# A second buffer for the transposed rope pages, and the next entry's page transposes ahead of the score mask

## The reference, cut to what matters

```python
c_past = cache_kv_latent[i][page_table].reshape(db, past, KV_LORA)
kr_past = cache_k_rope[i][page_table].reshape(db, past, ROPE_DIM)
s_past = einsum('bthc,bsc->bhts', q_abs, c_past) + einsum('bthr,bsr->bhts', q_rope, kr_past)
s = concatenate([s_past, s_new], -1) * scale          # s_new: the new token itself
p = softmax(s)
o_lat = einsum('bhts,bsc->bthc', p[..., :past], c_past) + einsum('bhtu,buc->bthc', p[..., past:], c_new)
```

## Time and profile before

| | |
|---|---|
| median of 3 runs | 1068.41 us (1066.91 to 1068.78) |
| span of the profiled execution | 1064.8 us; the profile gives no other time for that execution |
| PE busy | 990.8 us, 93% of the span |
| VectorE busy | 668.9 us, 63% |
| ScalarE busy | 387.6 us, 36% |
| GpSimd busy | 69.0 us, 6%, nearly all of it the gathers |
| chain that ended last | PE 78%, VectorE 12%, ScalarE 2% |

### The profile page before, as it was taken

How to read it: one execution, slowest core, us unless ns; L and a number is a source line. 1 busy time by engine, 2 the same in 40 slices (tenths; PEclk the granted TensorE clock), 3 DMA queues, 4 the chain that set the end, 5 groups by cost and what they waited for, 6 DMA issues and landing times.

```text
span 1064.8 us, 22625 instructions
## 1 busy us (share of the span) xinstructions
PE 990.8 (93%) x9310; PEld 913.0 (86%) x9310; DVE 668.9 (63%) x1052; ACT 387.6 (36%) x854; POOL 69.0 (6%) x76
## 2 busy tenths in 40 slices
PE   4999999999999996777789999999999999999995
PEld 3899999978888884454469999999999999999995
DVE  7558654765564556666565748798764244767567
ACT  3323433323233242121332313356562113656321
POOL 0000000000000033444400000000000000000000
PEclk9999999999999998789999999999999999999998
DMA  8522356040405167777816664142333342241633
GB/s 247 163 68 76 102 143 158 5 120 22 120 21 146 40 198 258 235 261 259 261 53 231 210 171 111 49 118 82 88 89 89 89 119 79 80 114 53 181 110 131
DMA packets 179381, 137.09 MB, mean 129 GB/s; under 512 B 19219, under 2 KB 163448, under 8 KB 179032
## 3 DMA queue, kind: packets, MB, share of 16 engines
q1 hardware_dynamic: 166442, 93.56, 31.4%
q0 software_dynamic: 10368, 37.75, 10.7%
q10 hardware_dynamic: 2502, 4.78, 1.2%
HBM read 124.27 MB, written 11.90 MB: 128 GB/s over the span
## 4 chain that ended last, share of the span: by engine, by line
PE 78%; DVE 12%; issue 4%; another core or an unknown queue 2%; ACT 2%; DMA 1%; ACTq 0%; DVEq 0%
PE PS L1958 34%; PE PS L2185 9%; PE PS L2632 8%; PE PS L2694 6%; PE PS L1969 3%; PE PS L2528 3%; PE PS L2356 3%; PE PS L2411 2%; DVE pages_T L1431 2%; DVE w_lo L1173 2%; PE PS L2223 2%; PE PS L2212 1%; PE PS L2200 1%; PE PS L2284 1%
## 5 line engine op out<-in xcount | busy, mean ns | idle before, releaser
L1958 PE MATMUL PS<-x_hi,w_hi 128*128 128x268 f32 x744 | 164.5, 293 | 2.7 <-DVE x_lo L1220 1.4
L1173 DVE TENSOR_TENSOR w_lo<-w_raw,w_hi 128x2048 fp32r<-128x2048 f32 (+3 forms) x65 | 125.9, 1936 | 60.6 <-ACT w_hi L660 48.8
L1958 PE MATMUL PS<-x_hi,w_lo 128*128 128x268 f32 x744 | 160.2, 287 | 0.0
L1958 PE MATMUL PS<-x_lo,w_hi 128*128 128x268 f32 x744 | 160.2, 287 | 0.0
L660 ACT ACTIVATE w_hi<-w_raw 128x2048 fp32r<-128x2048 f32 (+3 forms) x59 | 94.5, 1601 | 149.5 <-PE PS L1958 90.2
L1958 PEld LDWEIGHTS PS<-x_hi,w_hi 128*128 128x128 f32 x744 | 120.3, 189 | 6.0 <-issue 2.4
L1958 PEld LDWEIGHTS PS<-x_lo,w_hi 128*128 128x128 f32 x744 | 119.7, 189 | 0.0
L1958 PEld LDWEIGHTS PS<-x_hi,w_lo 128*128 128x128 f32 x744 | 119.4, 189 | 0.0
L2185 PE MATMUL PS<-x_hi,w_hi 128*128 128x268 f32 x256 | 78.5, 307 | 0.0
L611 POOL DMA_INDIRECT pages_c<-in_cache_kv_latent_dram,page_rows x48 | 46.4, 966 | 426.9 <-DVE w_uk_T L1478 372.6
L2356 PE MATMUL PS<-pages_T,q_blocks 128*32 128x128 f32 x1024 | 49.0, 297 | 26.2 <-issue 15.9
(11 more groups left out here) (373 smaller groups left out, 2311.7 us busy)
## 6 DMA issues: line engine op xcount, KB each, us to landing
w_raw<-in_w_ffn_in_dram SPq DMA_DIRECT2D x44, 512.0 KB, 4.5
w_raw<-in_w_in_dram SPq DMA_DIRECT2D x37, 512.0 KB, 7.0
w_raw<-in_w_ffn_out_dram SPq DMA_DIRECT2D x28, 320.0 KB, 3.7
w_raw<-in_w_o_dram SPq DMA_DIRECT2D x12, 512.0 KB, 6.3
w_raw<-in_w_ffn_out_dram SPq DMA_DIRECT2D x16, 384.0 KB, 4.1
gate_scratch<-gate_out ACTq DMA_DIRECT2D x8, 536.0 KB
gates<-gate_scratch SPq DMA_DIRECT2D x8, 536.0 KB, 8.9
x_T_scratch<-x_sum_T SPq DMA_DIRECT2D x1, 2144.0 KB, 7.6
```

Of the source, the lines that this page charges most:

```text
L1173: V.tensor_tensor(WL[:, par, 0:nk], RAW[:, par, 0:nk], WH[:, par, 0:nk].bitcast(F32), ALU.subtract).then_inc(s_wsplit, 1)
L1958: last = T.matmul(PS[:, bank, 0:HALF], w[:, par, k, m * P:(m + 1) * P], x[:, k0 + k, half * HALF:(half + 1) * HALF], start=start and k == ...
```

## The change

It adds a second tensor for the transposed rope rows, `RTT1`, in a part of the split weights' buffer that is free in this stage, and uses the two in turn. The rope transpose of entry b + 1 then waits only for the halves of entry b - 1. In VectorE's order the rope transpose and page 4 of the next entry move ahead of the mask, page 5 goes between column maximum and row maximum, and pages 6 and 7 go ahead of latent_out; in the last entry, which has no next one, the order stays. PE reads the rope tensor that belongs to its entry. The orders of the other engines are as they were, and no instruction is added or removed on them.

```diff
+        RTT1 = nc.alloc_sbuf_tensor_at("rope_T_odd", [P, 4, NCH, 32], F32,
+                                       offset=base + 2 * KT * COLS * 4 + (8 + 2 * ((19 + 1) % 2)) * slot_half)
+
+        def rope_T(b):
+
+            return RTT1 if b % 2 else RTT
...
             def turn_rope(b):
                 dve.wait_ge(S[f"rope_pages{b % 2}"], 16 * (1 + b // 2))
-                if b:
-                    dve.wait_ge(S["half_scored"], 2 * b)
-                V.transpose(RTT[:].rearrange("p r c i -> p c r i"), PGR[:, b % 2].rearrange("p (c r) d -> p c r d", r=4)).then_inc(S["rope_turned"], 1)
+                if b >= 2:
+                    dve.wait_ge(S["half_scored"], 2 * (b - 1))
+                V.transpose(rope_T(b)[:].rearrange("p r c i -> p c r i"), PGR[:, b % 2].rearrange("p (c r) d -> p c r d", r=4)).then_inc(S["rope_turned"], 1)
...
                 if more:
                     for c in range(4):
                         turn_chunk(b + 1, c)
+                    turn_rope(b + 1)
+                    turn_chunk(b + 1, 4)
                 scores_back(par, b)
                 if more:
-                    turn_rope(b + 1)
+                    turn_chunk(b + 1, 5)
                 max_rows(par)
                 if more:
-                    turn_chunk(b + 1, 4)
-                    turn_chunk(b + 1, 5)
+                    turn_chunk(b + 1, 6)
+                    turn_chunk(b + 1, 7)
                 else:
...
                 if b:
                     latent_out(1 - par, b - 1)
-                if more:
-                    turn_chunk(b + 1, 6)
-                    turn_chunk(b + 1, 7)
                 inv_sum(par)
...
-                        pages = CT[:, r, k, 4 * a:4 * a + 4, :] if k < 8 else RTT[:, r, 4 * a:4 * a + 4, :]
+                        pages = CT[:, r, k, 4 * a:4 * a + 4, :] if k < 8 else rope_T(b)[:, r, 4 * a:4 * a + 4, :]
```

## The result

The changed kernel takes 1078.71 us (median of 12 runs, 1073.62 to 1081.51) where the kernel before takes 1069.26 in the same comparison: ratio 1.0069, 95% interval 1.0048 to 1.009. It is slower, by 7.4 us by the ratio (the two medians are 9.5 us apart), and lies above the whole forecast range. The profiled execution has a span of 1079.5 us, 14.7 more than that of before; it is one of the slower executions (1081.51 us), and the one shown of before is the fastest of its three (1066.91 us). The traces therefore show more loss than the medians do, 1.6 to 2 times as much.

The account below looks back on a forecast made before the run. No engine is full: a ring of waits sets 18 us per cache entry, with PE holding 78% of the chain. 0.3 - 1.0 + 3 x 0.2 + 1.4 = +1.3 on 1068.4 gives 1069.7 us, range 1067.5 to 1071.8.

Parts of the forecast that it names:

- five in a row: After a second score half, gathers of pages 4 and 5 follow the three without a gap; last starts 509.2, not 506.7.
- the hold: While gathers follow each other, PE's results hardly come out, until 1.8 to 1.9 us after the last gather's start.
- The cycle from 507.36: Entry 4's second half to entry 5's: forecast +0.2 us, as for each of three such cycles.
- the slower rival: Held weigh chunks delay the third gather of a cycle's second burst: 1.0 us more in three cycles, 1072.7 us; chance 0.20.
- cycle 1 to 2: Entry 1's second half to entry 2's: no wait to remove, burst may end one spacing sooner; 0 to -1.24, taken -1.0 us.
- The later burst: Gathers of pages 0 to 2, each waiting for its weigh chunk: first at +13.6 us, third at +16.1.
- the table's two sums: Changes of the seven entry-to-entry cycles added up: +13.5 us measured, +1.3 us forecast.
- The last cycle: From 521.01, no gathers in its second half, VectorE bounds; six transposes before the mask: +1.4 us, row maximum at +20.4.
- only the waits go: Rival: the two added gathers do not lengthen what PE feels, PE's waits for transposes go: -4.2 us, 1064.2; chance 0.22.
- Entry 0: First cycle: a gather now starts near its max_turn; 0 to +1.0 us, taken +0.3.
- the second rival: No longer delay of PE's results by gathers, and second score halves shrink too: -8.2 us, 1060.2; chance 0.11.

Follow-up runs that it names:

- early gathers only: The kernel before, with only the gathers of pages 5 and 6 let go two transposes sooner: 1076.27 us, ratio 1.0041 on the slower sort.
- the held-back kernel: The changed kernel with the gathers of pages 5 to 7 waiting until after the row maximum: 1064.77 us, ratio 0.9977 on the slower sort.
- the kernel in which only the waits go: The kernel before, with pages 6 and 7 transposed ahead of latent_out and nothing else moved: 1068.68 us, ratio 0.998 on the slower sort.
- quarter gathers: The changed kernel, gathers of entries 3 to 7 fetching 1 KB per partition instead of 4: 1076.9 us, 1.005 on the slower sort.

## Why the prediction was wrong

**The first step that failed is "five in a row".** The size of the hold was read about rightly. With five gathers the forecast put the exponentials near +9.5, and the kernel with early gathers only starts them at +9.29, +8.81 and +8.86 in its three cycles with five unbroken gathers. (In its two others a pause stands behind the second gather, and they start at +6.84 and +9.08, the last gather at +7.0 in both: the last gather alone doesn't set the hold.) But in the changed kernel six came. The prediction let page 7's gather wait for a row maximum behind the burst (the earlier trace rows have it at 508.55, +5.95, after the burst); the row maximum came at +5.58, inside it, and with pages 6 and 7 now directly behind, the sixth gather left at +7.53. The same prediction says that results hardly come out in a burst; one that does was enough, and the sum had no case for it. Nor was max_spread held back until +8.85: PE dispatched it at +6.94, in the burst, and only its result came late.

The sixth gather is not the whole of it. The cycle from 507.36 missed its forecast by 2.1 us, of which it explains some 0.8; and five gathers alone already cost 4.4 us in the kernel with early gathers. The rest are terms that the sum put at nothing, or at a gain: the clock, the weigh chunks' late signals (which only the slower rival had) and the burst of cycle 1 to 2.

**What the longer hold brings on was not in the sum at all: the clock.** In the cycle from 507.36, term by term: max_spread's result +10.1 where its forecast dispatch at 8.85 gives +9.3 (0.42 us later, as at 509.14 and 509.56 in the kernel before), some 0.8 us late; latent_turn at a clock of 0.50 took 1.02 us (0.61 in the held-back kernel's trace), which brings sum_spread to +13.0 instead of +11.8; weigh chunks 0 and 1 took 1.94 instead of 1.07. The later burst then began at +15.4 instead of +13.6.

**The slower rival's mechanism is there.** It was to decide above 2.5 us from the first to the third gather of the later burst. They start at 522.79 and 526.54, 3.75 us apart: weigh chunk 2 runs from 523.02 to 524.08, its signal comes 1.66 us late, at 525.74 by the semaphore events, and the gather that waits for it starts at 526.54. So the third gather is at +19.2 (forecast 16.1) and the second half ends at +20.7 (forecast 18.65, the rival's 19.65). The rival had the sign and this piece; its 1072.7 lacks the sixth gather and the clock.

**Cycle 1 to 2 was given a gain, -1.0, and lost 2.7.** The prediction looked only at its later burst. The long burst after the second half of entry 1 comes there too, six gathers up to +7.9, with max_spread's result at +10.4; it was simply not counted. This is the largest single miss, 3.7 of the 12.2 us between the table's two sums.

**The last cycle** was put at +1.4 and is +4.7 in this execution (19.7 and 19.8 us in two others of the same kernel, and 17.00, which is +2.0, in one whose burst has the pause). The reason given, six transposes ahead of the mask, holds: the row maximum of entry 6 is at 551.29, +23.2 after 528.09, with +20.4 forecast and +18.97 before (the last of the transposes, at 547.94, also waited 0.41 us for PE). But the row it starts from, inv_sum, is itself late by the same hold and clock: 541.70, +13.6, with +11.75 forecast.

```profile
541.70 0.21 DVE L1548 RECIPROCAL sm<-PS 128x8 f32<-128x8 f32 x1 [0.24 <-PE PS L2397]
541.82 4.58 DVE L1437 STREAM_TRANSPOSE pages_T<-pages_c 128x1024 f32<-128x1024 f32 x4
...
547.94 1.25 DVE L1437 STREAM_TRANSPOSE pages_T<-pages_c 128x1024 f32<-128x1024 f32 x1 [0.41 <-PE PS L2361]
...
551.29 0.28 DVE L1540 TENSOR_REDUCE sm<-PS 8x1 f32<-8x128 f32 x1 [0.38 <-PE PS L2388]
```

**What was right:** the wait on `pages_T` is gone; mask, column maximum and row maximum are not later for the transposes ahead of them; and the removed waits turn into something else. This last holds even without a longer burst: "only the waits go" gave -4.2 us, and the kernel in which only the waits go gains 2.1. There the later burst, of three gathers, starts at +12.7, where before one of four started at +11.8, and PE's second half ends, as before, 2.4 to 2.9 us after its last gather (488.40 behind 485.91). It is the burst that the end hangs on, not the transposes. Entry 0 (+0.3, measured +0.4) was right by luck: its cycle is 14.4 us in three other executions of the changed kernel, and 15.0 and 15.4 in the two of the kernel before.

**The rule of the Trainium skill** ("SBUF — State Buffer", section "SBUF: two separate sides"), by which ports of engines and of DMA do not contend, would have given the second rival's 1060.2. That the hold of an unbroken burst doesn't change with the bytes (+10.09 against +10.01) agrees with the rule; that PE is held all the same, on some machines, it leaves unexplained.

**What stays open.** What in a gather instruction holds PE's results, and why some machines don't show it: the three groups of runs without the changed kernel met the faster sort and all those with it the slower one, so the changed kernel was never timed on the faster sort, only its variants (quarter gathers 0.9979), and it can't be excluded that the sort goes with something other than the machine. Held-back gathers differ there from the kernel before by -0.1 to +0.2%, with intervals that reach +0.5%, so VectorE's new order by itself costs nothing that these runs can tell from none. How much of the 7.4 us is the hold and how much the clock that follows it was not taken apart. PE's own stops without a cause in the profile hardly grow: in the stage they sum to 19.4 us before, and in four executions of the changed kernel to 20.9 to 24.2, but to 26.0 in the kernel with pages 6 and 7 ahead alone, which loses nothing. So they alone do not make the loss.

The best kernel of the study is the changed one with the gathers held back: 0.23% faster than before where PE is held (0.07 to 0.39%), not distinguishable from it where it isn't.

## What to carry to other kernels

When an instruction moves, ask first which waits it satisfies on other queues. Here transposes, moved for PE's sake, released three gathers on GpSimd 3.0 to 4.8 us sooner, and these cost more than the transposes' lateness had. If a queue's instructions disturb another engine while they run back to back, keep its waits as they are when everything around it gets faster, or tighten them on purpose. And a stall of PE costs more than its length where the clock falls behind it: read the granted clock of the stretch after a stall, before putting the stall into a sum.

## What the runs showed of the hardware

- On machines where the kernel before takes 1069 us, PE's results come out late while gathers follow each other on GpSimd: max_spread's by 2.8 us after its modelled end, behind a burst of six. On machines where it takes 1034 us, max_spread's result came at +4.9 us in the midst of eleven gathers in a row; PE stops there up to three times beside gathers, for up to 2.2 us. PE's stops without a cause in the stage sum to 19.4 us in the kernel before on the slower sort, to 5.2 in the early-gathers kernel and 0 with quarter gathers on the faster. A gather takes 0.94 us on both. The difference is 3% of the whole kernel; in the stage of the entries the early-gathers kernel has cycles of 11.4 to 16.2 us there, and 14.3 to 20.4 on the slower sort.
- The hold behind six unbroken gathers is the same with a quarter of each gather's bytes (cycle 20.55 against 20.68 us, traffic 73 against 230 GB/s). Where the burst has a pause it was shorter with a quarter (+5.9 and +6.6 against +8.65 to +8.86 us).
- After a stretch in which PE was busy for 1.69 of 4 us, the granted clock was 0.50, the 1.2 GHz level, for the next eight us, in which PE was busy for 7.80.
